# Output projection of a hybrid encoder step: from float32 products to three one-pass products of split operands

## The reference, cut to what matters

```
x = x + g1 * (merged @ w_o)        # merged = gate_a * (a @ w_a) + gate_b * (b @ w_b)
h = rms_norm(x) * (1 + sc2) + sh2
x = x + g2 * hier_moe(h)           # 32 experts, top 2 of one group of 8 for each token
y = rms_norm(x) modulated again
```

## Time and profile before

| | |
|---|---|
| median of 3 runs | 968.44 us (968.15 to 968.72) |
| profiled execution, span | 963.2 us; the runs' median is 5.3 us longer |
| TensorE matmuls busy | 845.6 us, 88% of the span |
| VectorE / ScalarE / GpSimd busy | 509.0 / 190.9 / 168.8 us |
| mean granted TensorE clock | 0.940 of full speed |
| HBM read | 199.49 MB, 223 GB/s over the span |
| output projection with its transposes | 547.3 to 613.1 us |
| expert stage | from 661.9 us |

### The profile page before, as it was taken

The page is one execution under the profiler, slowest core; times in us unless marked ns, Lnnn a source line. Parts: engine busy times, 40 slices in busy tenths (PEclk is TensorE's granted clock), DMA queues, the critical chain, the costliest instruction groups (busy, mean ns, idle before and its releaser), DMA issues. The chain is left out here.

```text
span 963.2 us, 12133 instructions
## 1 busy us (share of the span) xinstructions
PE 845.6 (88%) x4994; PEld 618.5 (64%) x4994; DVE 509.0 (53%) x753; ACT 190.9 (20%) x284; POOL 168.8 (18%) x156
## 2 busy tenths in 40 slices
PE   2899999999998879979999999917999987979776
PEld 1688886347997879978878644605666655545432
DVE  1328999999999443351365543481333331222236
ACT  3211211111233121741120011201111110101003
POOL 1000000000045454143223000001122221121110
PEclk9899999999998889989999999856999998989899
DMA  9923225011332131365999593242999999999936
GB/s 323 315 64 88 65 67 174 1 44 44 89 88 57 48 88 45 88 219 175 316 314 322 186 381 149 97 193 83 411 404 416 415 418 394 368 406 394 373 110 248
DMA packets 112600, 204.16 MB, mean 212 GB/s; under 512 B 9484, under 2 KB 68212, under 8 KB 104350
## 3 DMA queue, kind: packets, MB, share of 16 engines
q1 hardware_dynamic: 94192, 159.36, 46.5%
q10 hardware_dynamic: 12830, 34.93, 9.6%
q0 software_dynamic: 5520, 9.06, 2.5%
HBM read 199.49 MB, written 14.84 MB: 223 GB/s over the span
## 5 line engine op out<-in xcount | busy, mean ns | idle before, releaser
L858 PE MATMUL PS<-arena 128*64 128x256 f32 (+1 forms) x1056 | 148.7, 411 | 30.2 <-issue 25.7
L1280 DVE SCALAR_TENSOR_TENSOR arena<-arena,VT 128x574 f32<-128x574 f32 x240 | 175.1, 811 | 0.0
L858 PEld LDWEIGHTS PS<-arena 128*64 128x64 f32 (+1 forms) x1056 | 108.8, 156 | 65.4 <-issue 36.9
L1695 POOL TENSOR_TENSOR wL<-arena,wH 128x1024 fp32r<-128x1024 f32 x32 | 83.2, 2621 | 360.8 <-ACT wH L998 360.8
L552 PE MATMUL PS<-arena 128*128 128x272 f32 x512 | 119.1, 396 | 1.6 <-DVE arena L1242 1.6
L552 PEld LDWEIGHTS PS<-arena 128*128 128x128 f32 x512 | 98.3, 192 | 22.1 <-issue 1.6
L619 PE MATMUL PS<-gH,wH 128*128 128x272 f32 x384 | 83.0, 299 | 9.1 <-POOL wL L1695 5.5
L1591 DVE TENSOR_TENSOR arena<-PS,arena 128x256 f32<-128x256 f32 x19 | 8.1, 424 | 140.1 <-ACT arena L1114 140.1
L619 PE MATMUL PS<-gL,wH 128*128 128x272 f32 x384 | 81.9, 296 | 0.0
L619 PE MATMUL PS<-gH,wL 128*128 128x272 f32 x384 | 81.7, 294 | 0.0
L878 PE MATMUL PS<-arena 128*64 128x512 f32 (+1 forms) x264 | 69.1, 597 | 1.4 <-DVE arena L1595 1.4
(11 more groups left out here) (282 smaller groups left out, 996.9 us busy)
## 6 DMA issues: line engine op xcount, KB each, us to landing
arena<-w_gate SPq DMA_DIRECT2D x32, 1024.0 KB, 7.3
arena<-w_up SPq DMA_DIRECT2D x32, 1024.0 KB, 15.4
arena<-w_down ACTq DMA_DIRECT2D x28, 1024.0 KB, 13.9
arena<-w_in SPq DMA_DIRECT2D x40, 512.0 KB, 5.2
arena<-w_ada SPq DMA_DIRECT2D x8, 2048.0 KB, 14.4
vecs<-w_ada SPq DMA_DIRECT2D x4, 2048.0 KB, 9.3
arena<-x_prompt SPq DMA_DIRECT2D x8, 512.0 KB, 8.0
arena<-w_in SPq DMA_DIRECT2D x4, 1024.0 KB, 6.3
```

The lines of the kernel that those rows point to most:

```text
L858: last = pe.matmul(PS[h * rows:(h + 1) * rows, 2, n * DE:(n + 1) * DE], hG[:, b, k * SLOTS + h * rows:k * SLOTS + (h + 1) * rows], buf[r / ...
L1280: dve.scalar_tensor_tensor(out=total, in0=src, scalar=tap, in1=total, op0=ALU.mult, op1=ALU.add).then_inc(conv_step, 1)
L1695: pool.tensor_tensor(wL2[q % 2][:, m], WP[q % 2][:, m], wH2[q % 2][:, m], ALU.subtract).then_inc(gw_split, 1)
```

## The change

The output projection takes its operands in split form. `mH` and `mL` are the high and low parts of `mT`, `wHO[hf]` and `wLO[hf]` those of the halves of `w_o`. `mL` is written over `mT` and `wLO` over the loaded weights; `mH` takes the place of the gates in `O_A`, `wHO` lies in `O_S` and `O_C`. ScalarE makes the high parts (`high_m`, `high_o`), VectorE the low parts of `mT` and of the first half of each weight tile (`low_m`, `low_o`), GpSimd the other half. `project` becomes 24 one-pass matmuls instead of 8 float32 ones, and starts with `project(0, 0)` before all of `mT` is merged, waiting block by block. `project_sample` becomes 48 one-pass matmuls, both halves into rows 0 to 31 of PSUM. The order becomes (0,0), (1,0), (2,0), (0,1), (1,1), with the rest as before. `gn2b` moves to another region, the sample's `g1b` is loaded for 32 rows instead of 64, and all four fixed expert sets are loaded after `project_sample`, since their region is now taken until then.

```diff
@@ SyncE
-                        g_rows = P if s == 0 else 2 * NSAMPLE
-                        sp.dma_start(g1b[s][0:g_rows, :], mod_vec(2, g_rows, s)).then_inc(mb_in, 16)
+                        sp.dma_start(g1b[s][0:rows, :], mod_vec(2, rows, s)).then_inc(mb_in, 16)
...
-            sp.wait_ge(hist_ps, 2)
...
+            sp.wait_ge(w_used, U_O + 2)
             load_first(0)
             load_first(1)
             sp.wait_ge(h2_ready, TT)
-            sp.wait_ge(w_used, U_O + 2)
             load_first(2)
             load_first(3)
@@ TensorE
-            full(pe, U_O)
-            pe.wait_ge(merged, KT)
-
-            def project(t, hf):
-                if t < 4:
-                    for k in range(KT):
-                        last = pe.matmul(PS[:, (2 * t + hf) % 8, :], mT[:, k, t * P:(t + 1) * P], W[hf][:, k, :],
-                                         start=(k == 0), stop=(k == KT - 1))
-                    last.then_inc(o_ps, 1)
+            def project(t, hf, first=False):
+
+                bank = (2 * t + hf) % 8
+                pe.wait_ge(ow_high, 2 * hf + 2)
+                for k in range(KT):
+                    if first:
+                        pe.wait_ge(m_high, k + 1)
+                    pe.matmul(PS[:, bank, :], mH[:, k, t * P:(t + 1) * P], wHO[hf][:, k, :], start=(k == 0), stop=False)
+                for k in range(KT):
+                    if first:
+                        pe.wait_ge(m_split, k + 1)
+                    pe.matmul(PS[:, bank, :], mL[:, k, t * P:(t + 1) * P], wHO[hf][:, k, :], start=False, stop=False)
+                for k in range(KT):
+                    if k % 4 == 0:
+                        pe.wait_ge(ow_split[k // 4], hf + 1)
+                    last = pe.matmul(PS[:, bank, :], mH[:, k, t * P:(t + 1) * P], wLO[hf][:, k, :], start=False, stop=(k == KT - 1))
+                last.then_inc(o_ps, 1)
 
             def project_sample():
                 pe.wait_ge(o_drained, 2)
-                for k in range(KT):
-                    for hf in range(2):
-                        last = pe.matmul(PS[NSAMPLE * hf:NSAMPLE * (hf + 1), hf, :], mT[:, k, NPROMPT:T], W[hf][:, k, :],
-                                         start=(k == 0), stop=(k == KT - 1))
+                for hf in range(2):
+                    for n, (part, w) in enumerate(((mH, wHO), (mL, wHO), (mH, wLO))):
+                        for k in range(KT):
+                            last = pe.matmul(PS[0:NSAMPLE, hf, :], part[:, k, NPROMPT:T], w[hf][:, k, :],
+                                             start=(n == 0 and k == 0), stop=(n == 2 and k == KT - 1))
                 last.then_inc(w_used, 2)
...
-            project(0, 0)
+            pe.wait_ge(dve_drained, KT + NGATE - 1)
+            project(0, 0, True)
+            pe.wait_ge(dve_drained, KT + NGATE)
             project(1, 0)
-            full(pe, U_O + 1)
+            pe.wait_ge(mod_added, NB)
+            project(2, 0)
             project(0, 1)
             project(1, 1)
             turn_h2(0)
-            pe.wait_ge(mod_added, NB)
-            project(2, 0)
             project(2, 1)
@@ ScalarE
+            def high_m(j):
+                act.wait_ge(merged, j + 1)
+                act.activation(mH[:, j, :], mT[:, j, :], ACT.Copy).then_inc(m_high, 1)
+
+            def high_o(hf):
+                full(act, U_O + hf)
+                for k in range(0, KT, 4):
+                    act.activation(wHO[hf][:, k:k + 4, :], W[hf][:, k:k + 4, :], ACT.Copy).then_inc(ow_high, 1)
+
+            for j in range(KT - 2):
+                high_m(j)
+            act.wait_ge(mod_ps, NB)
+            high_o(0)
+            for j in range(KT - 2, KT):
+                high_m(j)
+            act.wait_ge(w_used, U_O)
+            high_o(1)
@@ VectorE
+            def low_m(j):
+                dve.wait_ge(m_high, j + 1)
+                dve.tensor_tensor(mL[:, j, :], mT[:, j, :], mH[:, j, :], ALU.subtract).then_inc(m_split, 1)
+
+            def low_o(hf):
+                dve.wait_ge(ow_high, 2 * hf + 1)
+                dve.tensor_tensor(wLO[hf][:, 0:4, :], W[hf][:, 0:4, :], wHO[hf][:, 0:4, :], ALU.subtract).then_inc(ow_split[0], 1)
...
                 if 4 <= j < 4 + NB:
                     add_bias(j - 4)
+                if j >= KT + 2:
+                    low_m(j - KT - 2)
+            low_o(0)
+            for j in range(KT - 2, KT):
+                low_m(j)
+            low_o(1)
@@ GpSimd
             for q in range(4, 16):
                 low_gate(q)
+            for hf in range(2):
+                pool.wait_ge(ow_high, 2 * hf + 2)
+                pool.tensor_tensor(wLO[hf][:, 4:8, :], W[hf][:, 4:8, :], wHO[hf][:, 4:8, :], ALU.subtract).then_inc(ow_split[1], 1)
```

More of the change, by code:

```diff
@@ L98, in build @@
         wL2 = [split_parts(f"wL2{s}", O_W + 4096 * s, 2, KT, P) for s in range(2)]
+        mH = split_parts("mH", O_A, KT, T)
+        mL = split_parts("mL", O_V, KT, T)
+        wHO = [split_parts(f"wHO{s}", at, KT, BLK) for s, at in enumerate((O_S, O_C))]
+        wLO = [split_parts(f"wLO{s}", O_W + 4096 * s, KT, BLK) for s in range(2)]
         def halves_of(at, n):
@@ L148, in build @@
         sh2b = [view(O_H + 2048, D), view(O_H + 3072, D)]
-        gn2b = view(O_A + 12288, D)
+        gn2b = view(O_H, D)
         h2 = view(O_H, 2, D)
@@ L259, in build @@
         o_ps, o_drained = sem("o_ps"), sem("o_drained")
+        m_high, m_split = sem("m_high"), sem("m_split")
+        ow_high, ow_split = sem("ow_high"), [sem("ow_split0"), sem("ow_split1")]
         mb_in, mb2_in = sem("mb_in"), sem("mb2_in")
@@ L1410, in _ @@
                     if t < 4:
-                        dve.wait_ge(o_ps, (1, 3, 2, 4)[2 * t + hf] if t < 2 else 2 * t + hf + 1)
+                        dve.wait_ge(o_ps, (1, 4, 2, 5, 3, 6, 7, 8)[2 * t + hf])
                     else:
                         dve.wait_ge(w_used, U_O + 2)
-                    cols, r0 = slice(hf * 512, (hf + 1) * 512), NSAMPLE if (t, hf) == (4, 1) else 0
-                    dve.tensor_tensor(mg[0:w, cols], PS[r0:r0 + w, (2 * t + hf) % 8, :], g1b[s][r0:r0 + w, cols], ALU.mult).then_inc(o_drained, 1)
+                    cols = slice(hf * 512, (hf + 1) * 512)
+                    dve.tensor_tensor(mg[0:w, cols], PS[0:w, (2 * t + hf) % 8, :], g1b[s][0:w, cols], ALU.mult).then_inc(o_drained, 1)
                 dve.wait_ge(o_drained, 2 * t + 2)
```

## The result

The kernel became slower: 980.2 us (978.83 to 982.6, 4 runs) beside 968.3 us (967.84 to 968.72, 4 runs) of the kernel before, a ratio of 1.013, with a 95% interval of 1.0108 to 1.0153. The forecast was 970.2 with a range up to 972.3, so 10 us are missing from its sum. The profiled span is 978.3 us, 15.1 more than the 963.2 of before.

The account below looks back on a forecast made before the run. The projection was taken as TensorE-bound, its end setting the kernel's end. 10.0 us less work and 1.0 less old wait against 12.8 new wait (7.8 + 3.1 + 1.9) gave 1.7 later: 970.2 us, range 965.3 to 972.3.

Parts of the forecast that it names:

- The early ones hide: Branch loop before the projection: splitting `mT` tiles 0 to 4 fits VectorE's 3.85 us idle before each merge, costing nothing.
- nothing ahead of them is edited: Argument against the rival "The merge wins the port": the terms deciding its 0.35 us race lie behind unedited code.
- the race for the port: At the last merge: GpSimd's `low_o(0)` starts 0.35 us before VectorE's merge and makes it wait.
- A 512-column pass: Output projection on TensorE: each one-pass matmul takes 0.216 us, bounds 0.2146 and 0.226, so 10.0 us of work go.
- Port: Last merge on VectorE waits for the end of GpSimd's `low_o(0)`: 4.2 us lost, bounds 0 and 4.7.
- The merge wins the port: Rival at the last merge: GpSimd goes second, only `low_m(5)` is held; sample ends 0.7 us earlier; chance 0.18.
- Clock: First product of the projection: TensorE's idle time halves its clock once, losing 1.9 us (1.6 to 2.2).
- The clock falls twice: Rival: a second fall at TensorE's 2.4 us wait for h2 costs 1.2 us more, 971.3 us; chance 0.20.
- the 3.2 us at half rate: Lower bound for TensorE's work at half clock in the first product; 3.2 to 4.4 us loses 1.6 to 2.2.
- The waits for h2: TensorE behind `project(0,1)`: idle 2.4 us for the first h2 and 0.7 for the next, 3.1 together.
- Half 1 of the weights: Load and split of `w_o` half 1 before `project(0,1)`: off the path, with 3.6 and 2 us of cover.
- the expert loads: Four fixed expert sets loaded behind the sample product: 35 us of DMA, done by 650, 13 us of cover, cost nothing.

Follow-up runs that it names:

- The series: Low parts of `mT` from step 12, plus 15 series of 24 unread one-pass matmuls of 128 to 512 columns behind the sample product: 1030.4 us, one run.
- the low parts later: Also called `mL` later: the change with VectorE's subtractions for `mL` starting at step 12 of the branch loop instead of step 10; 971.0 us, ratio 1.005.
- the high parts first: The change with ScalarE making `high_m(0)` and `high_m(1)` before copying the last weight unit instead of behind it; 971.1 us, ratio 1.0047.
- the last one with GpSimd behind the merge: The change as it is, with GpSimd's `low_o(0)` also waiting for the last merge; 982.8 us, ratio 1.0148.
- the phases kernel: On GpSimd behind the merge: first three products as high x high, high x low, low x high, `low_m(5)` to `low_m(7)` behind `low_o(0)`; 965.6 us, again 966.0.
- the last two kernels: The phases kernel measured again (966.0 us), and the phases kernel with `project(2, 1)` ahead of the h2 transposes of tile 0 (961.9 us).
- GpSimd behind the merge: The low parts later, with GpSimd's first split of `w_o` also waiting for the last merge; 970.2 us, ratio 1.004.
- the version after it: The phases kernel with `project(2, 1)` ahead of tile 0's h2 transposes and tile 1's between `project(3, 0)` and `project(3, 1)`; 961.9 us, ratio 0.9951.

## Why the prediction was wrong, point by point

**The failed step: "The early ones hide: ScalarE and VectorE split `mT` tiles 0 to 4 in the 3.85 us that VectorE is idle before each merge."** The 3.85 us are real, and the subtraction of 0.70 us would have fitted. What I didn't do is ask where `high_m(0)` stands in ScalarE's list. I priced the work of the early parts and not the place of their waits: the change adds a wait on VectorE for ScalarE, at a time when ScalarE waits 14 us for a load. It cost 9.2 us, and two different ways of taking it away win back all of them. No rival of mine had it; they all began after the last merge, and the remark in one of them that "nothing ahead of them is edited" is wrong: the change puts `high_m` and `low_m` ahead of the last merge. Without the stall the kernel runs at 971, close to the 970.2 of the forecast, but that is luck: it is 4.7 us above the kernel before in its own measurement, where 1.7 was forecast, and it gets there with slower products and with the race for the port won, which the forecast had lost.

**"A 512-column pass ... I take 0.216; ... upper 0.226": mis-sized, it measured 0.232.** I held the extra 12 ns of the 272-column row for a constant. The series shows that it grows with the columns, 0.45 ns for each, against 0.42 for each in a float32 pass (0.2146 us). Had I scaled the row of 272 columns by 512/272, I would have had 0.237. The prompt's groups save 1.30 us each and not 1.68, and the sample product costs 4.2 more instead of 3.4: 6.2 us less TensorE work instead of 10.0. The Trainium skill (TensorE: Matmul & The Clock Gate, section "Back-to-back issue gap") gives N / 2.4 + 2.5 ns for an isolated matmul at full clock, 0.216 us at 512 columns, and about 0.131 us for a stream of weight loads and matmuls; the one-pass float32r products of this kernel, 0.232 us, follow neither.

**Port: right in kind and size.** The merge took 4.70 us, forecast as 4.9, and it does wait until GpSimd's instruction ends, also when that has twice the elements. That the race would be lost was a guess at 0.35 us: GpSimd was ahead by 0.43 and 0.36 us in the two profiles of the change, and the merge by 0.85 and 0.89 in those of the low parts later and the high parts first. So the rival "The merge wins the port" is real, and which of the two comes hangs on the load of the weights. In the traces of the change, of both kernels without the stall and of the last one with GpSimd behind the merge, the VectorE instruction of 128x544 with two SBUF inputs that meets GpSimd ends 0.58 to 0.59 us after it; `add_bias`, with one operand in PSUM, went through beside GpSimd at its usual 2.13 us. The rule of the Trainium skill that the prediction cited (SBUF — State Buffer, section "SBUF: two separate sides") is borne out by both. The exchange of the order is worth 2.1 us, forecast 2.4.

**Clock: right in kind, smaller in size.** PEclk was 0.50 from 564 to 570. The 9 matmuls left behind the last `mL` took 3.4 us (570.44 to 573.81) where 2.1 are due: 1.3 lost, forecast 1.9. No second fall came at the 2.13 us wait for h2, nor at 2.40 in the first profile of the phases kernel. But the rival "The clock falls twice" is not refuted: behind the waits of 2.55 and 2.27 us of the last two kernels PEclk was 0.50, from 583 to 586 and from 587 to 589. One reading of the earlier trace rows was off: the window from 315 to 316 has 0.53, where a fall at 315.5 would give 0.75, so the clock fell near 315.1. And no row shows the 3.2 us at half rate that the prediction took as its lower bound.

**The waits for h2** were 2.13 and 0.17 (forecast 2.4 and 0.7): with a slower product there is less to wait for. Half 1 of the weights and the expert loads were hidden, as forecast; the DMA engines were 0.97 busy from 629 to 658 us, right behind the sample product, and 0.44 from 658 to 666, well before tile 1 at 677.7; the moved loads alone gave 0.999.

The stage again with measured terms: 1.7 forecast, 3.8 for the work, less 0.8 for the waits, 0.6 for the clock and 0.4 for an earlier `mL`, is 3.7, and the trace has 3.6. Together with 9.2 that is 12.8, beside 11.9 in the medians.

**What stays open.** The kernels without the stall lie 3.9 to 4.8 us above the kernel before in the medians, while their stretches from the last merge to the sample product are longer by 1.6 (GpSimd behind the merge), 1.7 (`mL` later) and 2.7 us (high parts first). Some 2 to 3 us are in no stretch that I can name, and the phases kernel has no such remainder. The stretch from step 10 to the last merge is not it (41.2 us in all), and what follows the sample product takes 348.3 to 351.2 us in the profiles, 350.1 in the kernel before, with no order by version; the median of one set of runs and the profile of one execution can't be set against each other more closely. The ranks of versions within 3 us of each other are known from the intervals alone.

## What to carry to other kernels

When an edit puts a wait on one engine for another, look at what that other engine is doing at that moment, not only at how long the awaited instruction takes: walk up its list to the instruction ahead, and if that waits for a DMA, what is left of its wait is inherited. Work moved into an engine's idle time is free only if its inputs are ready within that time. And scale a row by columns before adding a constant to it, or keep both as bounds.

## What I had not expected of the hardware

A one-pass float32r product costs 0.45 ns a column, 8% more than one pass of a float32 product (0.2146 us for 512): three one-pass products are 5.56 us where a float32 one is 6.86, so the saving is 19% and not a quarter.

Executions differ by up to 6 us in code that no version edits: the merge of step 10 stands at 505.28 in the profile of the kernel before and at 511.45 in that of the change with GpSimd behind the last merge, and at 508.45 and 505.87 in the two of the change itself. The same window of the branch loop, untouched by every version, in the second run of the phases kernel and in the version after it:

```profile
400.00:500.00 100.00, 88.42 (x664) 78.10 (x663) 47.73 (x58) 33.24 (x47) 29.24 (x12) 0.93 0.68 226
```

```profile
400.00:500.00 100.00, 88.43 (x689) 77.00 (x687) 48.95 (x60) 33.24 (x47) 29.20 (x12) 0.98 0.70 232
```

The granted clock is 0.93 in one and 0.98 in the other, with 664 and 689 matmul records; the last merge then stands at 550.14 and 548.02. Of twelve profiles, the two kernels' own and those of the ten runs, nine have 0.93 to 0.95 and three 0.98, among them one of the change itself, so it doesn't follow the edit. The three with 0.98 have the merge of step 10 at 505.9 to 506.8, the six with 0.93 at 509.0 to 511.5, and the three with 0.95 at 505.3 to 508.7. That this is what sets the groups some 4 us apart in the times is argued, not shown.
